# RWKV scan: one product of constants, 384 columns at full height, at each step of the chain

## The chip, the cores and the metric

The kernel runs as one program on one core of a Trainium2 chip. The metric is the device time of one execution in microseconds (us). Three runs of the kernel before took 2750.27, 2752.72 and 2759.83 us; the median is 2752.72. All data are 32-bit floats.

The engines: TensorE (PE) multiplies matrices and writes into PSUM, which has 8 banks of 512 columns on 128 partitions. VectorE (DVE) and ScalarE (ACT) work element by element, GpSimd (POOL) and SyncE (SP) issue transfers here. TensorE's matmuls need a load of weights first (PEld in the profile). A product of 32-bit operands appears as two MATMUL records.

## The reference

The model has two hybrid blocks, then a block with an RWKV mixer and one with latent attention. The change lies in the scan of the RWKV mixer: 512 tokens (256 of context, then 256 of input), 16 heads of 64, two directions. What it computes, cut to the core:

```python
def wkv_scan(r, logw, k, v, a, b, s0):
    tm = lambda t: jnp.moveaxis(t.astype(jnp.float32), 2, 0)

    def step(s, inp):
        r_t, lw_t, k_t, v_t, a_t, b_t = inp
        sa = jnp.einsum('dbhij,dbhj->dbhi', s, a_t)
        s = s * jnp.exp(lw_t)[..., None, :] + sa[..., None] * b_t[..., None, :] + v_t[..., None] * k_t[..., None, :]
        return s, jnp.einsum('dbhij,dbhj->dbhi', s, r_t)

    s_fin, y = lax.scan(step, s0, (tm(r), tm(logw), tm(k), tm(v), tm(a), tm(b)))
    return jnp.moveaxis(y, 0, 2), s_fin
```

## The kernel before

`stage_rwkv_scan` works through 8 rounds of 128 channels (n = 0 to 7), each with two heads (e) and two directions (d). The 512 tokens are cut into NCK = 16 chunks of LCH = 32. For each round, products of small tiles turn every chunk into a matrix GR that carries a state over the chunk; then a chain of steps c = 0 to 16 runs the state through the chunks in order.

The order of all work is a list, `scan_order`, which every engine walks in the same order and picks its own part from. For round i it has two parts. In the first, the solving of round i (`atok`, `akv`, `pq`, `gr`) is mixed with the gram products of round i + 1 and the reading out of round i - 1. In the second, the chain of round i is mixed with the triangular inverse of round i + 1 on VectorE (`inv`, 31 pieces, from 0.3 of the chain on) and with the preparation of round i + 2: two pairs of LoRA products (`lora`, L1553), sums, a small transpose and a spread for the norm of kk (`kk`, L1538, L1696, L1544) and two scans on VectorE. Rounds 0 to 5 have a later round i + 2 to prepare, rounds 6 and 7 have none, and round 7 has no inverse either.

A step c of the chain on TensorE: it waits for `u_done`, the scaling of step c - 1; `carried` (L1641) adds GR times the scaled state U to the bank c % 2 and raises `state_up`; `inner` (L1634) opens the other bank, (c + 1) % 2, with the part of the next chunk that needs no state; `read_state` (L1649) and `read_inner` (L1658) write the outputs of the chunk into banks 2 and 3. VectorE meanwhile waits for `state_up`, multiplies columns 0 to 127 of the bank by the decay (`rw_u`, L1965) and raises `u_done`. All these products use quarters of the array: 64 rows by 64 columns of weights, with 64 or 32 columns streamed, four to a group. The state's banks are k.psum[0] and k.psum[1]; the chain uses 128 of their 512 columns, and nobody reads the others while the chain runs.

`k.con` holds constants in SBUF: the identity in columns 0 to 127 (`ident`), all ones in the next 128, and a block matrix of ones in the next.

Of the kernel before, what the change touches and what calls it, by code (L numbers as in the profile page):

```python
# [20 lines left out]
P = 128  # L21
# [105 lines left out]
def const(k, name):  # L127
    return k.con[:, CON[name]:CON[name] + P]
# [1225 lines left out]
def stage_rwkv_scan(nc, k, a, lora, kept, o):  # L1354
# [14 lines left out]
    with ExitStack() as ctx:  # L1369
# [56 lines left out]
        ident, headones = const(k, "ident"), const(k, "headones")  # L1426
# [18 lines left out]
        def rows64(i):  # L1445
            return slice(64 * i, 64 * i + 64)
# [73 lines left out]
        def _(pe):  # L1520
# [108 lines left out]
            def inner(n, c):  # L1629

                h, c2 = c % 2, c // 2
                for d in range(2):
                    for e in range(2):
                        mm = pe.matmul(k.psum[h][rows64(e), 64 * d:64 * d + 64], BG[n % 2][d][rows64(h), c2, e, 0:64],  # L1634
                                       PQ[d][rows64(h), c2, e, 64:128], start=(d == 0), stop=(c == 0), skip_group_check=True)
                return mm

            def carried(n, c):
                for d in range(2):
                    for e in range(2):  # L1640
                        mm = pe.matmul(k.psum[c % 2][rows64(e), 64 * d:64 * d + 64], GR[d][rows64(e), c, 0:64],  # L1641
                                       U[rows64(e), c % 2, d, :], start=False, stop=True, skip_group_check=True)
                return mm

            def read_state(n, c):
                for d in range(2):
                    at = 256 * d + 32 * (c // 2)
                    for e in range(2):
                        mm = pe.matmul(k.psum[2 + c % 2][rows64(e), at:at + 32], U[rows64(e), c % 2, d, :],  # L1649
                                       GR[d][rows64(e), c, 64:96], start=(d == 0), stop=False, skip_group_check=True)  # L1650
                return mm

            def read_inner(n, c):
                h, c2 = c % 2, c // 2
                for d in range(2):
                    at = 256 * d + 32 * c2
                    for e in range(2):
                        mm = pe.matmul(k.psum[2 + h][rows64(e), at:at + 32], PQ[d][rows64(h), c2, e, 64:128],  # L1658
                                       BG[n % 2][d][rows64(h), c2, e, 64:96], start=(c == 0 and d == 0), stop=True,
                                       skip_group_check=True)  # L1660
                return mm

            def chain(n, c):
                if c == 0:
                    pe.wait_ge(gr_down, 8 * (n + 1))
                    if n:
                        pe.wait_ge(u_done, (NCK - 1) * n)
                        pe.wait_ge(ysum_done, n)
                        pe.wait_ge(step_up, (NCK + 1) * n)
                    inner(n, 0).then_inc(state_up, 1)  # L1670
                    inner(n, 1).then_inc(step_up, 1)
                    return
                pe.wait_ge(step_up, (NCK + 1) * n + c)
                if c < NCK:
                    pe.wait_ge(u_done, (NCK - 1) * n + c)
                    if c < NCK - 1:
                        carried(n, c).then_inc(state_up, 1)
                    if c + 1 < NCK - 1:
                        inner(n, c + 1)
                    read_state(n, c)  # L1680
                read_inner(n, c - 1).then_inc(step_up, 1)
# [7 lines left out]
            for item in items:  # L1689
# [33 lines left out]
                elif kind == "pq":  # L1723
                    solved(n, *item[2:])
                elif kind == "gr":
                    steps_made(n, *item[2:])
                elif kind == "chain":
                    chain(n, item[2])
                elif kind == "bonus" and item[2] == 0:
                    bonus_sums(n)  # L1730
                elif kind == "read" and item[2] == 1:
                    pe.wait_ge(ysum_done, n + 1)
                    pe.matmul(take(*item), cen, ysb, start=True, stop=True).then_inc(yc_up, 1)
                    free(ysq_done, n + 1, *item)
                elif kind == "read" and item[2] == 2:
                    pe.wait_ge(ysq_done, n + 1)
                    out = take(*item)
                    for q in range(4):
                        mm = pe.matmul(out[:, 2 * q:2 * q + 2], ysq[:, q * P:(q + 1) * P], half2[:, 0:2], start=True,
                                       stop=True)  # L1740
                    mm.then_inc(var_up, 1)
                    free(var_down, n + 1, *item)
                elif kind == "read" and item[2] == 3:
                    pe.wait_ge(yr_done, n + 1)
                    out = take(*item)
                    pe.transpose(out[0:8, 0:P], rst, ident).then_inc(yt_up, 1)
                    free(yt_down, n + 1, *item)
                elif kind == "read" and item[2] == 4:
                    pe.wait_ge(yt_down, n + 1)
                    spread(take(*item), rstT).then_inc(yb_up, 1)  # L1750
                    free(o_done, n + 1, *item)
# [825 lines left out]
```

## Time and profile before

| | us |
|---|---|
| median of three runs | 2752.72 |
| lowest, highest | 2750.27, 2759.83 |
| the profiled execution | 2753.79 |
| its span, first to last instruction | 2752.1 |
| TensorE busy with matmuls | 2289.5 (83%) |
| TensorE busy with weight loads | 1798.2 (65%) |
| VectorE busy | 983.9 (36%) |
| ScalarE busy | 523.1 (19%) |

Durations of single pieces come from the profiled execution, so sums are made against its 2753.79 us. Its mean granted TensorE clock is 0.848 of full speed. The scan takes the stretch from about 1700 to 2375 us. In the profile, "matmuls cover" means that at least one matmul was under way; several on different quarters of the array can overlap. Line numbers L... are those of kernel.py as below. "64\*64" ahead of a shape says how many rows and columns of the array a matmul used.

### The profile page before, as it was taken

Reading aid. Unit: us, or ns where it says so; the run is one execution under the profiler, and the core shown is the slowest. Engines: PE = TensorE matmul, PEld = TensorE weight load, DVE = VectorE, ACT = ScalarE, POOL = GpSimd, SP = SyncE. Lnnn points to the kernel's source line nnn. Section 1 sums busy time; section 2 is a strip of 40 time slices with the busy share of each in tenths; the row PEclk is TensorE's granted clock in tenths of the full one; section 3 lists DMA queues with packets and bytes.
Section 4 is the critical chain, followed back from the end, with each engine's and each line's share of the span. In section 5 each row is a group of like instructions: output and inputs, shape, how many; then the busy total and the mean of one; then the engine's idle time right before and its main releaser. Section 6 shows DMA issues by size and latency. Waiting matters only on the chain. (4 is left out here: it accounts for less than half of the span.)

```text
span 2752.1 us, 43845 instructions
## 1 busy us (share of the span) xinstructions
PE 2289.5 (83%) x18934; PEld 1798.2 (65%) x18934; DVE 983.9 (36%) x2209; ACT 523.1 (19%) x944; POOL 57.5 (2%) x84
## 2 busy tenths in 40 slices
PE   1999955798999876999579973988889889779797
PEld 1888854687888765888534432777777778536445
DVE  3224345402440562773341005335443343110243
ACT  1011122401000102000100013344433442000142
POOL 0000010000000300000000000000000000000000
PEclk9999977998999988999889985666756666689889
DMA  7455411325874311874212211111111110312100
GB/s 290 178 227 228 168 50 27 66 100 204 319 270 153 122 46 61 319 306 184 96 51 97 77 52 41 35 42 33 24 40 33 43 25 10 123 65 92 42 20 16
DMA packets 101929, 301.25 MB, mean 109 GB/s; under 512 B 71272, under 2 KB 79720, under 8 KB 83568
## 3 DMA queue, kind: packets, MB, share of 16 engines
q1 hardware_dynamic: 93808, 223.01, 24.0%
q0 software_dynamic: 7936, 75.50, 7.1%
q8 instruction: 149, 2.44, 0.4%
q14 instruction: 36, 0.29, 0.0%
HBM read 284.78 MB, written 13.71 MB: 108 GB/s over the span
## 5 line engine op out<-in xcount | busy, mean ns | idle before, releaser
L263 PE MATMUL bank<-h,ring 128*128 128x256 f32 x2944 | 646.5, 383 | 22.8 <-DVEq L967 15.3
L263 PEld LDWEIGHTS bank<-h,ring 128*128 128x128 f32 x2944 | 566.2, 192 | 104.0 <-DVEq L967 16.1
L263 PE MATMUL bank<-mixed,ring 128*128 128x512 f32 x384 | 165.0, 592 | 1.3 <-DVE mixed L1249 1.3
L877 PE MATMUL bank<-ffn_hidden,ring 128*128 128x256 f32 x704 | 152.4, 379 | 3.3 <-PEq L903 3.3
L877 PEld LDWEIGHTS bank<-ffn_hidden,ring 128*128 128x128 f32 x704 | 133.6, 190 | 22.2 <-issue 4.1
L263 PEld LDWEIGHTS bank<-mixed,ring 128*128 128x128 f32 x384 | 72.9, 190 | 93.5 <-issue 91.4
L156 DVE CUSTOM_DVE_ANT_0 next_w<-next_w,next_vec,par 128x1024 f32<-128x1024 f32 x96 | 120.3, 1281 | 11.3 <-DMA next_w<-in_mod_stream 11.3
L1658 PE MATMUL bank<-ring 64*64 64x32 f32 x1024 | 110.3, 289 | 0.6
L1634 PE MATMUL bank<-ring 64*64 64x64 f32 x960 | 99.3, 300 | 8.3 <-ACT rw_gr L1856 8.3
L1649 PE MATMUL bank<-rw_gr,rw_u 64*64 64x32 f32 x960 | 98.4, 283 | 0.5
L1658 PEld LDWEIGHTS bank<-ring 64*64 64x64 f32 x1024 | 93.3, 208 | 1.7 <-PE bank L1658 1.7
L1641 PE MATMUL bank<-rw_u,rw_gr 64*64 64x64 f32 x896 | 75.1, 315 | 22.5 <-DVE rw_u L1965 18.2
L889 DVE SCALAR_TENSOR_TENSOR x<-bank,mod,x 128x256 f32<-128x256 f32 x24 | 10.0, 477 | 231.6 <-PE bank L877 231.6
L1597 PE MATMUL bank<-ring 32*32 32x128 f32 x1024 | 89.0, 341 | 4.0 <-DMA ring<-rw_mt_kept 2.2
L1965 DVE TENSOR_TENSOR rw_u<-bank,rw_lam 128x128 f32<-128x128 f32 x120 | 34.8, 290 | 153.8 <-PE bank L1641 95.6
L1641 PEld LDWEIGHTS bank<-rw_u,rw_gr 64*64 64x64 f32 x896 | 55.4, 205 | 52.4 <-issue 28.7
L1597 PEld LDWEIGHTS bank<-ring 32*32 32x32 f32 x1024 | 74.2, 137 | 20.8 <-issue 14.4
L1634 PEld LDWEIGHTS bank<-ring 64*64 64x64 f32 x960 | 79.3, 195 | 9.7 <-ACT rw_gr L1856 9.3
L1649 PEld LDWEIGHTS bank<-rw_gr,rw_u 64*64 64x64 f32 x960 | 83.2, 206 | 1.5 <-PE bank L1658 1.5
L877 PE MATMUL bank<-y,ring 128*128 128x256 f32 x384 | 83.1, 379 | 0.8 <-PEq L679 0.8
L401 DVE COPY y<-bank 128x512 f32<-128x512 f32 x20 | 13.8, 692 | 186.1 <-PE bank L263 186.1
L877 PEld LDWEIGHTS bank<-y,ring 128*128 128x128 f32 x384 | 72.9, 190 | 10.9 <-issue 1.1
(362 smaller groups left out, 3353.9 us busy)
## 6 DMA issues: line engine op xcount, KB each, us to landing
ring<-in_stream SPq DMA_DIRECT2D x89, 2048.0 KB, 8.1
next_w<-in_mod_stream POOLq DMA_DIRECT2D x24, 2048.0 KB, 10.3
ctx<-in_mod_rest POOLq DMA_DIRECT2D x16, 1024.0 KB, 7.5
rwkv_projections<-proj_out POOLq DMA_DIRECT2D x8, 1024.0 KB, 6.7
rw_rkvg<-rwkv_projections SPq DMA_DIRECT2D x8, 1024.0 KB, 4.8
y<-bias_table SPq DMA_DIRECT2D x48, 128.0 KB, 4.8
rw_at<-rw_at_kept SPq DMA_DIRECT2D x16, 256.0 KB, 4.2
rw_at_kept<-ring SPq DMA_DIRECT2D x32, 64.0 KB, 1.9
```

What stands on the lines that cost most here:

```text
L156: return nc.vector.tensor_tensor_reduce(products, w, vec, 1.0, bias, ALU.mult, ALU.add, out)
L263: mm = pe.matmul(out, ring_tile(k, n, kt, i * P), rhs[kt], start=start and kt == kts[0], stop=stop and kt == kts[-1])
L401: nc.vector.tensor_copy(dst, k.psum[2 * (j % 2)].rearrange("p (i t) -> p i t", i=2)).then_inc(stored_dve, 1)
L877: mm = pe.matmul(k.psum[grp * 4 + i][:, 0:T], ring_tile(k, n, kt, i * P), rhs[part * KT + kt], start=(part == 0 and kt == 0), stop=(part = ...
L889: nc.vector.scalar_tensor_tensor(k.x[:, m, :], k.psum[m][:, 0:T], gain[:, m:m + 1], k.x[:, m, :], ALU.mult, ALU.add)
L1597: pe.matmul(out[brows(h), j * P:(j + 1) * P], BG[n % 2][d][brows(h), c2, e, 96:128], AV[brows(h), c2, e, :], start=True, stop=True)
L1634: mm = pe.matmul(k.psum[h][rows64(e), 64 * d:64 * d + 64], BG[n % 2][d][rows64(h), c2, e, 0:64], PQ[d][rows64(h), c2, e, 64:128], start=(d ...
L1641: mm = pe.matmul(k.psum[c % 2][rows64(e), 64 * d:64 * d + 64], GR[d][rows64(e), c, 0:64], U[rows64(e), c % 2, d, :], start=False, stop=Tru ...
L1649: mm = pe.matmul(k.psum[2 + c % 2][rows64(e), at:at + 32], U[rows64(e), c % 2, d, :], GR[d][rows64(e), c, 64:96], start=(d == 0), stop=Fal ...
L1658: mm = pe.matmul(k.psum[2 + h][rows64(e), at:at + 32], PQ[d][rows64(h), c2, e, 64:128], BG[n % 2][d][rows64(h), c2, e, 64:96], start=(c == ...
L1965: v.tensor_tensor(U[:, (c + 1) % 2, :, :], k.psum[c % 2][:, 0:P].rearrange("p (d v) -> p d v", d=2), lam[:, n % 2, :, c + 1:c + 2].to_broa ...
```

## The change

One line in `chain`: after `carried` of step c, and before `inner` of step c + 1, TensorE gets a product of the identity with 384 columns of the constants. It uses all 128 rows and columns of the array and writes columns 128 to 511 of the bank (c + 1) % 2, which nobody reads. It stands under the condition of `inner`, so in steps 1 to 13 of each round.

```diff
                     if c < NCK - 1:
                         carried(n, c).then_inc(state_up, 1)
                     if c + 1 < NCK - 1:
+                        pe.matmul(k.psum[(c + 1) % 2][:, P:512], ident, k.con[:, 0:384], start=True, stop=True)
                         inner(n, c + 1)
                     read_state(n, c)
                 read_inner(n, c - 1).then_inc(step_up, 1)
```

The order of TensorE's instructions at the start of a round's chain (L1641 `carried`, L1634 `inner`, L1649 `read_state`, L1658 `read_inner`, L1538 the sums of squares, L1553 a LoRA pair), before:

```order
458 L1538 MATMUL bank<-rw_half,rw_sq 128x2 x4
459 L1641 MATMUL bank<-rw_u,rw_gr 64x64 x4
460 L1634 MATMUL bank<-ring 64x64 x4
461 L1649 MATMUL bank<-rw_gr,rw_u 64x32 x4
462 L1658 MATMUL bank<-ring 64x32 x4
463 L1641 MATMUL bank<-rw_u,rw_gr 64x64 x4
464 L1634 MATMUL bank<-ring 64x64 x4
465 L1649 MATMUL bank<-rw_gr,rw_u 64x32 x4
466 L1658 MATMUL bank<-ring 64x32 x4
467 L1553 MATMUL bank<-lora,rw_w 128x512 x2
```

The same place with the change, where L1679 is the new product:

```order
458 L1538 MATMUL bank<-rw_half,rw_sq 128x2 x4
459 L1641 MATMUL bank<-rw_u,rw_gr 64x64 x4
460 L1679 MATMUL bank<-con 128x384
461 L1634 MATMUL bank<-ring 64x64 x4
462 L1649 MATMUL bank<-rw_gr,rw_u 64x32 x4
463 L1658 MATMUL bank<-ring 64x32 x4
464 L1641 MATMUL bank<-rw_u,rw_gr 64x64 x4
465 L1679 MATMUL bank<-con 128x384
466 L1634 MATMUL bank<-ring 64x64 x4
467 L1649 MATMUL bank<-rw_gr,rw_u 64x32 x4
468 L1658 MATMUL bank<-ring 64x32 x4
469 L1553 MATMUL bank<-lora,rw_w 128x512 x2
```

Nothing else moved: each step has its one product behind the state's four, and the other engines' orders are the same.

## Rows read from the trace of the kernel before

**Rows 1.** The page: TensorE's granted clock in tenths, 40 slices of the span.

```profile
PEclk9999977998999988999889985666756666689889
```

**Rows 2.** Stretches: from:to, length, busy time per engine (instructions), PEclk, DMA share, GB/s.

```profile
1758.00:2372.00 614.00, 544.97 (x10468) 470.20 (x10467) 256.42 (x754) 216.69 (x392) 0.00 (x0) 0.66 0.14 28
```

**Rows 3.** Line L1965, steps 1 to 14 of rounds 4, 2, 6 and 7.

```profile
L1965 DVE TENSOR_TENSOR rw_u<-bank,rw_lam x14: 266/292/293, 2101.8 to 2136.0; 128x128 f32<-128x128 f32 x14
...
L1965 DVE TENSOR_TENSOR rw_u<-bank,rw_lam x14: 266/292/292, 1933.5 to 1961.8; 128x128 f32<-128x128 f32 x14
...
L1965 DVE TENSOR_TENSOR rw_u<-bank,rw_lam x14: 291/292/293, 2274.6 to 2300.0; 128x128 f32<-128x128 f32 x14
...
L1965 DVE TENSOR_TENSOR rw_u<-bank,rw_lam x14: 291/292/292, 2344.8 to 2369.2; 128x128 f32<-128x128 f32 x14
```

**Rows 4.** In order of time, TensorE, round 4: start, length, instruction, count.

```profile
2099.95 1.17 PE L1538 MATMUL bank<-rw_half,rw_sq 128*128 128x2 f32 x8 [0.41 <-ACT rw_sq L1785]
2101.05 0.58 PE L1641 MATMUL bank<-rw_u,rw_gr 64*64 64x64 f32 x5
...
2103.04 0.37 PE L1641 MATMUL bank<-rw_u,rw_gr 64*64 64x64 f32 x2
...
2104.89 2.08 PE L1553 MATMUL bank<-lora,rw_w 64*128 64x512 f32 x4
2106.89 0.58 PE L1641 MATMUL bank<-rw_u,rw_gr 64*64 64x64 f32 x5
```

**Rows 5.** In order of time, round 7, steps 1 and 2.

```profile
2344.30 0.35 PE L1641 MATMUL bank<-rw_u,rw_gr 64*64 64x64 f32 x5 [0.45 <-DVE rw_u L1965]
...
2344.78 0.29 DVE L1965 TENSOR_TENSOR rw_u<-bank,rw_lam 128x128 f32<-128x128 f32 x1 [0.63 <-PE bank L1641]
...
2345.46 0.27 PE L1641 MATMUL bank<-rw_u,rw_gr 64*64 64x64 f32 x2
```

**Rows 6.** In order of time, VectorE, round 4, scalings of steps 8 to 14.

```profile
2119.66 0.29 DVE L1965 TENSOR_TENSOR rw_u<-bank,rw_lam 128x128 f32<-128x128 f32 x1
...
2124.72 0.29 DVE L1965 TENSOR_TENSOR rw_u<-bank,rw_lam 128x128 f32<-128x128 f32 x1
...
2126.82 0.29 DVE L1965 TENSOR_TENSOR rw_u<-bank,rw_lam 128x128 f32<-128x128 f32 x1
...
2130.07 0.29 DVE L1965 TENSOR_TENSOR rw_u<-bank,rw_lam 128x128 f32<-128x128 f32 x1
...
2134.68 0.29 DVE L1965 TENSOR_TENSOR rw_u<-bank,rw_lam 128x128 f32<-128x128 f32 x1
...
2136.02 0.29 DVE L1965 TENSOR_TENSOR rw_u<-bank,rw_lam 128x128 f32<-128x128 f32 x1
```

**Rows 7.** Stretches of rounds 2, 4, 7 and of 2155 us.

```profile
1940.00:1950.00 10.00, 9.33 (x214) 7.77 (x211) 6.72 (x27) 3.44 (x6) 0.00 (x0) 0.98 0.01 4
2101.00:2136.00 35.00, 31.81 (x455) 27.01 (x455) 18.66 (x66) 6.16 (x9) 0.00 (x0) 0.50 0.01 1
...
2155.00:2160.00 5.00, 5.00 (x126) 4.38 (x120) 1.78 (x3) 4.25 (x8) 0.00 (x0) 0.96 0.01 3
2344.00:2346.00 2.00, 1.63 (x54) 1.55 (x55) 0.49 (x3) 0.00 (x0) 0.00 (x0) 1.00 0.00 0
2350.00:2365.00 15.00, 14.48 (x246) 13.40 (x244) 2.04 (x7) 0.00 (x0) 0.00 (x0) 0.50 0.01 2
```

**Rows 8.** In order of time, TensorE, round 2, the LoRA pairs.

```profile
1936.62 2.08 PE L1553 MATMUL bank<-lora,rw_w 64*128 64x512 f32 x4
...
1943.01 0.27 PE L1641 MATMUL bank<-rw_u,rw_gr 64*64 64x64 f32 x2
...
1944.06 1.13 PE L1553 MATMUL bank<-lora,rw_w 64*128 64x512 f32 x4
1945.12 0.38 PE L1641 MATMUL bank<-rw_u,rw_gr 64*64 64x64 f32 x5
```

**Rows 9.** In order of time, TensorE, behind round 4's chain.

```profile
2144.86 0.39 PE L1566 MATMUL bank<-rw_xa,ring 64*64 64x64 f32 x4 [4.54 <-DVE rw_xa L1900]
...
2152.77 1.91 PE L1733 MATMUL bank<-rw_ysb,rw_cen 128*128 128x512 f32 x2
```

## The prediction

> **What bounds the kernel now.** I number the scan's eight rounds 0 to 7 and the steps of a round's chain c = 0 to 16. I began with the page: in its row of the granted clock, slices 25 to 35 of 40 are the one long stretch at 5 to 7 tenths [rows 1], and that is the scan. The table of stretches says how much: between 1758 and 2372 us, matmuls cover 545 of 614 us and the mean clock is 0.66 [rows 2]. The clock has two levels, 1.2 and 2.4 GHz, which the rows show as 0.50 and 1.00, so a mean of 0.66 is a third of the time high.
>
> Next the chain of one round, on VectorE, whose scaling (L1965) closes each step. Round 4 needs 34.2 us from step 1 to step 14, round 2 only 28.3, rounds 6 and 7 25.4 and 24.4 [rows 3]. The steps themselves come from the order of time on TensorE: at the low clock a plain step takes 2103.04 - 2101.05 = 1.99 us [rows 4], at the high clock 2345.46 - 2344.30 = 1.16 us [rows 5]. In both the engine hardly waits; the one wait for a scaling in these rows is 0.45 us in front of step 1 of round 7 [rows 5]. So in steps 1 to 8 TensorE sets the pace. From step 9 on, in rounds 0 to 5, it does not: VectorE works through the triangular inverse between the scalings, and 2.10, 3.25, 4.61 (for two) and 1.34 us pass between them, with no idle time of VectorE in front of them [rows 6]. There an extra product lies beside VectorE's work as far as TensorE's step stays shorter.
>
> When does the clock change? In round 7 it is high at first (1.00 in 2344 to 2346) and then 0.50, with matmuls in 14.5 of 15 us [rows 7]. The only wide products in the chains are the LoRA pairs (L1553, two in each of rounds 0 to 5): behind the one at 1936.62 the clock was 0.98 from 1940 to 1950, which makes round 2's short chain; behind the one at 2104.89 it did not rise, since 2101 to 2136 has a mean of 0.50 [rows 4, 7, 8]. It is 0.96 in 2155 to 2160, behind a product of 512 columns at full height that ran from 2152.77 to 2154.68 [rows 7, 9]. So small tiles alone did not bring it up; what stood before a rise was work over all rows of the array.
>
> The Trainium skill ("TensorE: Matmul & The Clock Gate", What's actually happening) says that the default is throttled and activity releases it. If busy time were what counts, rows 7 would show the high level; the trace disagrees, 0.50 with matmuls in 97% of the time, so what kind of matmul runs matters. By the page's rule read as it stands, the clock would follow any product put in; that is the third rival.
>
> **The change part by part.** One product per step 1 to 13, 13 x 8 = 104 in all, between the state's product (L1641) and the next step's inner products (L1634). It waits for nothing new and frees nothing; no DMA, no work of another engine. What queues behind it on TensorE: inner(c+1), the two reads, then the state's product of step c+1. The scaling of step c has its semaphore before it, so the product delays the scaling of step c+1, not of c.
>
> Price of one at each clock. The nearest row is the LoRA pair: two products of 512 columns, 64 rows each, side by side, thus a full-height one of 512. At the low clock the step that holds it takes 2106.89 - 2103.04 = 3.85 us, 1.86 more than the plain one [rows 4]; 384 columns are 0.75 of that, 1.40 us. At the high clock 1945.12 - 1943.01 = 2.11, 0.95 more [rows 5, 8]; times 0.75 is 0.71 us. Lower bound: no cost, where VectorE is late. Upper bound: the lone 512-column product, 1.91 us, and 0.2 for a weight load that isn't hidden, times 0.75 = 1.6 low, some 0.9 high [rows 9]. I take 1.40 and 0.71, since the pair stands in this very place of the chain. A plain step becomes 3.39 us low and 1.87 high. Note: high with the product is hardly shorter than low without it (1.99). The most that the change can win is therefore small.
>
> The skill's page "TensorEngine Tiling (Array Packing)" (Key Properties) adds that changing the tiling mode drains TensorE. The LoRA pair changes mode as well, so that its 1.86 us already hold it; if the full array cost one more drain each way, the upper bound would apply, some 20 us more in all.
>
> What the clock does. In rounds 0 to 5 it falls about step 0 (behind eight tiny products, L1538, in front of step 1 [rows 4]), before the first new product runs. Then the product is 1.40 us in a step of 3.39, less than the LoRA pair's 1.86 in 3.85 at 2104.89, which brought nothing: I expect no rise in steps 1 and 2. The first LoRA pair with new products on both sides is more full-height work than the pair at 1936.62, behind which it rose; so there I expect the rise. It then holds: the product is 0.71 us in a high step of 1.87. Between the scalings of steps 10 and 11 VectorE's 3.25 us leave TensorE idle for 1.4 us, and the clock may fall again, in about half the rounds. Rounds 6 and 7 arrive high and should stay.
>
> Sum for round 4, steps 1 to 14 (scaling to scaling): 3.39 low; 5.25 with the pair (3.85 + 1.40); 2.6 for the rise within the step; 1.87 twice; 2.82 (1.87 + 0.95); 1.87; 4.03 for the step with the spread L1544 (5.06 low [rows 6], less 0.83 for the plain step's gain, less 0.91 for the spread's, taken like the pair's 1.86 - 0.95, plus 0.71); 2.10, 3.25, 4.61 covered; 2.6 for the last, half high at 1.87, half low at 3.39. Together 36.3 against 34.2: +2.1. Rounds 0, 1, 3, 5 alike, so 5 x 2.1 = 10.5. Round 2 loses its luck: 36.3 - 28.3 = +8.0. Rounds 6 and 7: 13 x 1.87 = 24.3, against 25.4 and 24.4: -1. Sum +18.
>
> Some chain will not behave: a step of 3.39 us with its product repeats almost unchanged, so a round that misses the rise stays low. All low, it is ten steps of 3.39, two of 5.25 with pairs and one of 6.46 with the spread, 50.9 us: 16.7 more than before, 14.6 more than forecast. I count one such round in eight: +15. Behind the chain nothing is won: TensorE waits 4.54 us for VectorE there and is low again [rows 9].
>
> Forecast: 2753.8 + 18 + 15 = 2787 for the profiled execution. It took 2753.8 (span 2752.1 and 1.7 around it), 1.1 above the median of 2752.7; against that, 2786.
>
> **Rivals.**
> Low throughout: the products are never enough, pair or not. For it: the pair at 2104.89 brought nothing. Cost: rounds 0, 1, 3, 4, 5 each +16.7, round 2 50.9 - 28.3 = +22.6, rounds 6 and 7 13 x 3.39 = 44.1, +18.7 and +19.7; together +144: 2898. Against: the rise at 1940 came with less.
> Hidden: the clock as before and the products in TensorE's waits. Against: at the low clock the engine waits under 0.2 us a step (0.52 of 15 us over seven steps and a half [rows 7]), and 104 x 1.40 = 146 us don't go into that. A middle case stands here too: what the products cost is given back by the clock. Either ends within 8 us of before, 2745 to 2761.
> High throughout, and faster: the first product in step 1 already lifts or holds the clock in every round. Rounds 0 to 5 then take six plain ones of 1.87, two of 2.82, 4.03, and 9.96 for the covered ones, 30.9 with the last at 1.87 among the six: 5 x -3.3, round 2 +2.6, rounds 6 and 7 -1: -15, and with a product a tenth cheaper in some 80 steps another -5: 2734 to 2739. What decides it is step 1, whether the product's share at the low clock is enough. Against: it is under the LoRA pair's at 2104.89. The rule of the Trainium skill's page on TensorE's clock, named above, would come out at this same time.
>
> **How the numbers follow.** Partly high as forecast, from +8 to +80 according to how many rounds stay low (none to four of eight, and a product at its upper bound): 0.58. Low throughout or nearly: 0.10. Hidden or balanced: 0.15. High throughout: 0.17. A change of over 0.3% (8 us) is what this measurement can tell. So faster 0.17, same 0.15, slower 0.68. The range: 2738 takes in most of the high case, 2850 four or more rounds low; the likeliest case's own range is 2761 to 2833.
>
> **What would show it.** L1679 with 104 products, two records each; steps of 3.4 us with clock 0.50 and of 1.9 us with 1.00; in rounds 0 to 5 the change from the one to the other behind the first L1553; steps 9 to 13 unchanged; rounds 6 and 7 at 1.00. It is wrong if steps 1 and 2 already run in 1.9 us (then faster), if the pairs lift nothing, or if a high step takes over 2.1 us (the product dearer than 0.9).

## The result: 5% slower, and the profile after

The changed kernel takes 2888.31 us (median of four runs, 2881.24 to 2915.25) against 2754.94 for the one before (four runs, 2750.27 to 2759.83): a ratio of 1.0502, 95% interval 1.0429 to 1.0575. I had forecast 2786, range 2738 to 2850. The direction was right; the size is four times the forecast, and above the range. The profiled execution took 2894.58 (span 2892.9), 140.8 more than that of before.

The page shows the product as one group of 208 records, two for each of the 104, with no idle time in front of it. What answers to [rows 1] is the granted clock, which is at 5 to 8 tenths in slices 23 to 35.

```profile
PE 2444.7 (85%) x19142; PEld 1845.1 (64%) x19142; DVE 983.8 (34%) x2209; ACT 522.3 (18%) x944; POOL 57.3 (2%) x84
...
PEclk9999977999999978998899756675666866599889
...
L1679 PE MATMUL bank<-con 128*128 128x384 f32 x208 | 152.5, 831 | 0.0
...
L1634 PEld LDWEIGHTS bank<-ring 64*64 64x64 f32 x960 | 50.6, 185 | 107.7 <-issue 98.4
```

The last line is new: the weight loads of the inner products (L1634) now stand behind 98.4 us of idle time put down to "issue"; before, the whole group had 9.7 us in front of it, nearly all for ScalarE. This idle time isn't itself the price: E1 below has 0.6 us of it and still pays 0.73 us a step, and E9 has 89.3 us of it (in front of the loads of L1641) with a cheaper product.

The table of stretches for the scan (answering to [rows 2]) has it growing from 614 to 754 us, at a mean clock of 0.67, nearly what it was. That mean hides the change: it is now high in other places.

```profile
1758.00:2512.00 754.00, 697.26 (x10799) 513.07 (x10794) 256.54 (x754) 219.26 (x397) 0.00 (x0) 0.67 0.12 25
```

The scalings, now L1966, steps 1 to 14: round 2, round 4, round 6, round 7. They answer to [rows 3].

```profile
L1966 DVE TENSOR_TENSOR rw_u<-bank,rw_lam x14: 251/292/293, 1965.4 to 2020.0; 128x128 f32<-128x128 f32 x14
...
L1966 DVE TENSOR_TENSOR rw_u<-bank,rw_lam x14: 290/292/293, 2182.4 to 2226.7; 128x128 f32<-128x128 f32 x14
L1966 DVE TENSOR_TENSOR rw_u<-bank,rw_lam x14: 290/292/293, 2370.4 to 2418.6; 128x128 f32<-128x128 f32 x14
L1966 DVE TENSOR_TENSOR rw_u<-bank,rw_lam x14: 291/292/293, 2463.0 to 2511.5; 128x128 f32<-128x128 f32 x14
```

Round 2 went from 28.3 to 54.6 us, round 4 from 34.2 to 44.3, rounds 6 and 7 from 25.4 and 24.4 to 48.2 and 48.5. With step 0 to step 1 counted as well (from the scaling of step 0 to that of step 14), all rounds are:

```
us, scaling 0 to scaling 14       round 0     1     2     3     4     5     6     7    sum
before                            35.69 36.08 31.57 36.73 36.47 36.78 26.37 25.30  265.0
after                             56.95 40.80 56.39 57.45 47.83 40.84 49.09 49.38  398.7
```

That is +133.7. The stretches between the rounds add 2.9 (349.7 against 346.9), the first scaling comes 5.7 later, and 1.5 is won behind the last. So the change is in the chains, as forecast, and nearly nowhere else.

The clock in four stretches: round 7 from step 1 on; round 2, all its steps; round 1 behind its first LoRA pair.

```profile
2463.00:2511.00 48.00, 47.12 (x440) 30.13 (x442) 3.79 (x13) 0.00 (x0) 0.00 (x0) 0.50 0.00 1
...
1964.00:2020.00 56.00, 55.36 (x484) 34.88 (x485) 18.73 (x66) 6.16 (x9) 0.00 (x0) 0.51 0.01 1
...
1885.00:1905.00 20.00, 18.48 (x277) 12.00 (x277) 12.25 (x45) 3.43 (x5) 0.00 (x0) 1.00 0.01 2
```

Behind the first LoRA pair the clock rose in rounds 1, 4 and 5 and did not in 0, 2 and 3. Rounds 6 and 7 arrived high (step 1 takes 0.92 us in both) and fell in step 2. The order of time on TensorE, round 7 at the low clock, then round 4 at the high one:

```profile
2476.90 0.69 PE L1641 MATMUL bank<-rw_u,rw_gr 64*64 64x64 f32 x8
2477.52 1.65 PE L1679 MATMUL bank<-con 128*128 128x384 f32 x2
2479.10 0.40 PEld L1634 LDWEIGHTS bank<-ring 64*64 64x64 f32 x6 [1.08 <-issue]
...
2480.66 0.69 PE L1641 MATMUL bank<-rw_u,rw_gr 64*64 64x64 f32 x8
...
2196.60 0.45 PE L1641 MATMUL bank<-rw_u,rw_gr 64*64 64x64 f32 x8
2196.98 0.91 PE L1679 MATMUL bank<-con 128*128 128x384 f32 x2
...
2198.78 0.45 PE L1641 MATMUL bank<-rw_u,rw_gr 64*64 64x64 f32 x8
```

A step is 3.76 us low and 2.18 high. Against 1.98 and 1.16 of before the product costs 1.78 and 1.02; the forecast had 1.40 and 0.71. The same place in the kernel before shows what may lie behind a part of it:

```profile
2352.75 0.32 PE L1641 MATMUL bank<-rw_u,rw_gr 64*64 64x64 f32 x2
2352.78 0.31 PE L1634 MATMUL bank<-ring 64*64 64x64 f32 x1
```

There L1641 and L1634 run in turns. Now the product stands between the two: L1641 finishes by itself, and the first weight load of L1634 comes only at the product's end. In the rows of round 7 a low step of 3.76 us falls into 0.62 from the start of L1641 to that of the product, 1.58 from there to L1634, and 1.56 to the next L1641. So the product holds TensorE for 1.58 us, and the rest of the step takes 2.18 in place of 1.98.

### The profile page after: what moved, and what is told of

Read it like the earlier page. It is cut to its first block and busy times, and to the rows that moved or that the text cites. A ratio compares the mean times of both kernels' runs of the same rounds, so it can differ in the third digit from the quotient of the medians.

```text
span 2892.9 us, 44261 instructions
## 1 busy us (share of the span) xinstructions
PE 2444.7 (85%) x19142; PEld 1845.1 (64%) x19142; DVE 983.8 (34%) x2209; ACT 522.3 (18%) x944; POOL 57.3 (2%) x84
## 5 line engine op out<-in xcount | busy, mean ns | idle before, releaser
L1679 PE MATMUL bank<-con 128*128 128x384 f32 x208 | 152.5, 831 | 0.0
L1966 DVE TENSOR_TENSOR rw_u<-bank,rw_lam 128x128 f32<-128x128 f32 x120 | 34.8, 290 | 279.8 <-PE bank L1641 224.3
L1634 PEld LDWEIGHTS bank<-ring 64*64 64x64 f32 x960 | 50.6, 185 | 107.7 <-issue 98.4
L1658 PE MATMUL bank<-ring 64*64 64x32 f32 x1024 | 104.3, 279 | 0.6
L1649 PE MATMUL bank<-rw_gr,rw_u 64*64 64x32 f32 x960 | 94.4, 275 | 0.5
L1658 PEld LDWEIGHTS bank<-ring 64*64 64x64 f32 x1024 | 87.6, 197 | 1.7 <-PE bank L1658 1.7
L1649 PEld LDWEIGHTS bank<-rw_gr,rw_u 64*64 64x64 f32 x960 | 79.7, 196 | 1.5 <-PE bank L1658 1.5
L1599 PE MATMUL bank<-ring,con 32*32 32x64 f32 x1024 | 79.2, 275 | 0.0
L1641 PE MATMUL bank<-rw_u,rw_gr 64*64 64x64 f32 x896 | 70.8, 301 | 9.7 <-DVE rw_u L1966 4.5
L2066 PE MATMUL bank<-mla_h,ring 128*128 128x256 f32 (+1 forms) x240 | 67.3, 444 | 12.5 <-PEq L190 12.5
```

What stands on the lines that cost most here:

```text
L1599: mm = pe.matmul(out[krows(h), j * P + 64:(j + 1) * P], ident[krows(h), krows(h)], AV[krows(h), c2, e, 0:64], start=True, stop=True)
L1679: pe.matmul(k.psum[(c + 1) % 2][:, P:512], ident, k.con[:, 0:384], start=True, stop=True)
L1966: v.tensor_tensor(U[:, (c + 1) % 2, :, :], k.psum[c % 2][:, 0:P].rearrange("p (d v) -> p d v", d=2), lam[:, n % 2, :, c + 1:c + 2].to_broa ...
L2066: mm = pe.matmul(out, ring_tile(k, n, kt, i * P), rhs[kt], start=(kt == 0), stop=(kt == KT - 1))
```

## The experiments

Two questions were open: why the product is dearer than the forecast (a price of changing from 64x64 tiles to the full array and back, or the place), and why the clock did not rise, and fell in rounds 6 and 7. All times are medians (of two runs in E1 to E3, E5, E6, E8 and E9, of five in E4, four in E7, six in E10 and E11); each ratio is against the kernel before on the same chip, with its 95% interval. As the clock is not the same in every round, I read prices from single steps and behaviour from the rounds. "Low" and "high" are clock 0.50 and 1.00.

**E1, 8 columns in place of 384.** In the change's place:

```diff
+ pe.matmul(k.psum[(c + 1) % 2][:, P:P + 8], ident, k.con[:, 0:8], start=True, stop=True)
```

> The product as in the change, full height, but 8 columns instead of 384. Theory A (fixed price: at the low clock 1.78 us a product against 1.28 of streaming, so some 0.50 us go for the change of the array's mode and a load of weights that nothing hides): low steps of 1.99 + 0.50 = 2.5 us, some 104 x 0.5 less what VectorE covers, about +40 us, 2790. Theory B (the price goes with the columns, full height streams slower than 2 passes of 384 at 1.2 GHz): 8 columns cost nothing, steps of 2.0, 2755.

2824.13, ratio 1.0272 (1.0227 to 1.0317). The order of time in round 7, low:

```profile
2426.49 0.59 PE L1679 MATMUL bank<-con 128*128 128x8 f32 x2
...
2426.60 0.29 DVE L1966 TENSOR_TENSOR rw_u<-bank,rw_lam 128x128 f32<-128x128 f32 x1 [2.40 <-PE bank L1641]
...
2429.19 0.59 PE L1679 MATMUL bank<-con 128*128 128x8 f32 x2
```

A low step is 2.71 us: 0.73 for a product that streams next to nothing. So there is a fixed price in this place. From 8 to 384 columns a step grows by 1.05 us (2.71 to 3.76), just as the product's own row does (0.59 to 1.65), so the rest is the same at any width. The rows split the 0.73 us: 0.52 from the product's start to L1634, and 0.20 more in the rest of the step, as with 384 columns. The expectation, 0.50 us a product and 2790 us, was too low. The product doesn't bring the clock up either: every round is low from its third step on, as all but round 2 were before (35.6 and 35.8 us in rounds 6 and 7, 42.0 to 43.8 in the others, sum 330.0).

**E2 and E3, the same columns as 64x64 tiles.** In a step, between its wait for the reads of the step before (`step_up`) and that for the scaling (`u_done`); E3 has both calls, E2 one:

```diff
+ def fill(b, at, cols):
+     for e in range(2):
+         pe.matmul(k.psum[b][rows64(e), at:at + cols], ident[rows64(e), rows64(e)],
+                   k.con[rows64(e), 0:cols], start=False, stop=True, skip_group_check=True)
...
+ if 2 <= c < NCK - 1:
+     fill(c % 2, P, 384)
+     fill(c % 2, P, 384)
```

> In place of the full-height product, two products on quarters of the array that together cover all rows, 64 rows x 64 columns of weights, 384 columns streamed, side by side; no change of mode. They stand in steps 2 to 14 before the state's product. Theory A: 1.28 us and hardly more, low steps of 3.3 to 3.4, high ones of 1.85 to 1.9. Theory B: 1.78, steps of 3.76 and 2.18 again. On the clock: if the share of work over all rows in a step decides, the cheaper product has the larger share (1.28 of 3.35 against 1.28 of 3.76), and more rounds rise behind the LoRA pairs than the three of six that did. Time about 2790 to 2840 with A, 2885 with B.

> The two quarter products twice in each of steps 2 to 14. If the share of work over all rows decides on the clock: 2.56 of a low step of 4.6 us; the clock rises in every round within two or three steps, rounds 6 and 7 stay high, and steps 3 to 8 take some 2.5 us. Time near 2800, although twice as much was added. If the clock doesn't answer to these products: every step low, 4.6 us, some 2990.

E2: 2814.45, ratio 1.0237 (1.0196 to 1.0278). A low step is 3.27 (price 1.29), a high one 1.83 (0.66). E3: 2805.49, ratio 1.0204 (1.0158 to 1.0251): with twice the work no slower, though the 9 us between the two medians are within the noise. In E2 all of rounds 0 to 5 rose (0, 2, 4 and 5 behind the first LoRA pair, 1 and 3 behind the second), and rounds 6 and 7 ran low. One stretch of E2's round 7, one of E3's round 7:

```profile
2395.00:2430.00 35.00, 34.27 (x385) 23.96 (x384) 3.15 (x11) 0.00 (x0) 0.00 (x0) 0.50 0.01 1
```

```profile
2394.00:2419.00 25.00, 24.34 (x421) 15.93 (x415) 2.92 (x10) 0.00 (x0) 0.00 (x0) 1.00 0.01 2
```

TensorE is covered by matmuls to 98% and 97% in these two, and one is at the low level, the other at the high. In E3 every round rose by step 3. The busy share does not tell the levels apart. What differs between E2 and E3 is the wide work, by which I mean long products over all rows: once in a step it left rounds 6 and 7 low, twice it lifted them. Such work can be done in 64x64 tiles, so the full-height form isn't needed for it.

**E4, no product in the chain, one in each wait of step 0.** The waits of step 0 that concern other things are moved ahead of that for the masked Gram blocks (`gr_down`):

```diff
+ fill(3, 0, 384)
  pe.wait_ge(gr_down, 8 * (n + 1))
  inner(n, 0).then_inc(state_up, 1)
  inner(n, 1).then_inc(step_up, 1)
+ fill(3, 0, 192)
```

> No product in the steps at all; two pairs of quarter products per round in TensorE's waits around step 0: 384 columns while it waits for the last copy before the chain, 192 columns while it waits for the first scaling. Theory C (the clock falls because of the waits around step 0, and a chain of high steps of 1.16 us then holds itself): rounds 6 and 7 high throughout, 16 us instead of 25.4 and 24.4; rounds 0 to 5 high for some of steps 1 to 8, up to 6 us less each: 2710 to 2740. Theory D (the chain's small tiles can't hold the high clock, whatever stands before them): it falls in step 2 or 3 as before, 2750 to 2757.

2714.59, ratio 0.9863 (0.983 to 0.9896): 1.4% faster than the kernel before. Its profiled execution took 2749.2, the others 2707 to 2721, so its trace serves for single steps and rounds only. The products in round 4, in order of time; before, TensorE waited 0.98 us for ScalarE in front of this round's first L1634 and 0.41 us in front of L1538:

```profile
2113.66 0.86 PE L1665 MATMUL bank<-con 64*64 64x384 f32 x4
...
2115.00 0.53 PE L1665 MATMUL bank<-con 64*64 64x192 f32 x4
```

Rounds 2 and 4 took 26.9 us (high to step 8), round 6 21.5 and round 7 16.3; rounds 0, 1, 3 and 5, with 35.5 to 36.5, were within 1.3 us of before. So a round whose beginning is bridged can keep the high clock throughout, in round 7 with matmuls in 15.0 of 16 us and no wide work in any step.

```profile
2351.00:2367.00 16.00, 15.01 (x436) 13.53 (x435) 3.85 (x14) 0.00 (x0) 0.00 (x0) 1.00 0.01 3
```

**E5, E4 and the change's product together.** The edit is E4's with the change's line.

> The change's full-height products in steps 1 to 13, and the two pairs of quarter products in the waits around step 0. Theory E (in a low step of 3.76 us the product is too small a share to lift the clock, in a high one of 2.18 us it is enough to hold it, so a round keeps the clock it starts with): rounds 6 and 7 now high from start to end, 0.9 + 13 x 2.18 = 29.3 us each instead of 49.1 and 49.4; rounds 0 to 5 high from step 1 where they start high (about half of them, some 36 us). Time some 60 us less than the change: 2810 to 2840. Theory F (the full-height product itself brings the clock down, whatever the start): rounds 6 and 7 low again behind step 1, 49 us, 2880.

2789.67, ratio 1.0154 (1.0093 to 1.0215). Round 7's scalings and clock:

```profile
L1973 DVE TENSOR_TENSOR rw_u<-bank,rw_lam x14: 290/292/292, 2391.4 to 2419.7; 128x128 f32<-128x128 f32 x14
```

```profile
2391.00:2420.00 29.00, 28.13 (x466) 18.68 (x466) 4.08 (x14) 0.00 (x0) 0.00 (x0) 1.00 0.01 2
```

Rounds 6 and 7 are 29.2 us in place of 49.1 and 49.4, at the high clock to the end, with the very product that ran at the low clock in the changed kernel. Rounds 0 to 5 are 40.6, 34.8, 36.3, 34.8, 36.4 and 57.8: the first five were high in step 1 and stayed so at least to step 9, the last was low from its first step to its end. So with this product in it a chain can stay at either clock. In rounds 6 and 7 what stands before it decided which; to be high in step 1 isn't enough, since both were so in the changed kernel too. The time came out below the 2810 to 2840 of Theory E, as five of rounds 0 to 5 were high and not about half.

**E6, the change's line twice.**

> The change's product twice in each of steps 1 to 13. The second needs no new mode and no new weights: at the low clock + 1.28 us to the first's 1.78, steps of 5.04. If the share of full-height work in a step decides on the clock: 2.56 of 5.04 us is more than what failed (1.28 of 3.76, and 1.28 of 3.27 with quarters, rounds 6 and 7) and less than what rose (2.56 of 4.55, quarters twice). If it rises, steps of 2.8 us, rounds 6 and 7 about 38 us each, time near 2850, less than with half the work; if not, every step low at 5.04, rounds 6 and 7 66 us each, some 3040.

2835.23, ratio 1.032 (1.0279 to 1.0361): 53 us less than with the line once. A low step is 5.04 and a high one 2.82, so the second product adds 1.28 us low and 0.64 high, less than the first with 1.78 and 1.02. Every round was high by step 4 (rounds 6 and 7 39.0 and 37.6 us, sum 345.6).

```profile
2416.00:2450.00 34.00, 33.20 (x438) 21.29 (x434) 3.52 (x13) 0.00 (x0) 0.00 (x0) 1.00 0.01 1
```

**E7, E4 and one more product before step 1.** In `key_values`, before its waits, for the last of them:

```diff
+ if (d, e) == (1, 0):
+     if n:
+         pe.wait_ge(step_up, (NCK + 1) * n)
+     fill(0, P, 384)
```

> As e4_bridge (products only in the waits around step 0), and one more pair of quarter products, 384 columns, in TensorE's wait of 0.84 us before the key-value products of the second direction, where the clock fell in rounds 1, 3 and 5 of e4_bridge's profile and made their chains start low. Theory C: with that wait bridged all eight chains start high; rounds 0 to 5 take about 27 us to step 14 as rounds 2 and 4 did (26.9), 16.3 in round 7. Time 2680 to 2705, 10 to 30 below e4_bridge. Rival: the fall there has another cause than the wait (eight products of 8 rows stand there too), then as e4_bridge, 2715.

2712.54, ratio 0.9859 (0.9811 to 0.9906), no better than E4. Rounds 1 and 2 began high and lost it at step 3, round 3 at step 2, and round 4 began low (sum 239.9); round 1 as a whole:

```profile
1837.00:1869.00 32.00, 28.82 (x428) 24.12 (x426) 17.83 (x64) 5.84 (x8) 0.00 (x0) 0.53 0.01 2
```

The expectation failed: a high start isn't enough in rounds 0 to 5. What is missing there stays open. It can't be wide work alone: rounds 2 and 4 of E4 have the same steps and held the clock to step 8, and round 7 held it through all its steps (16.3 us) without any.

**E8, half the height.** 64 rows by 128 columns of weights, in the change's place:

```diff
+ r = (c + 1) % 2
+ pe.matmul(k.psum[r][:, P:512], ident[rows64(r), :], k.con[rows64(r), 0:384], start=True, stop=True)
```

> In the change's place, one product of 64 rows (those of the inner products behind it) and 128 columns of weights, 384 columns streamed. It changes the array's mode, but leaves the other rows free. If the change of mode costs the 0.50 us beyond streaming: low steps of 3.76 again. If it is the full height (nothing can be loaded or streamed beside it): below 3.4, since the other rows' work lies beside it. The clock: half the rows, a smaller share, so low throughout also behind the LoRA pairs; some 2860 to 2890.

2934.78, ratio 1.0682 (1.064 to 1.0725), above the 2860 to 2890 expected. A low step is 3.75 us, the same as with the full height, and the clock is low in all eight rounds, behind both LoRA pairs too (sum 440.7).

```profile
2511.45 1.64 PE L1680 MATMUL bank<-con 64*128 64x384 f32 x2
...
2515.19 1.64 PE L1680 MATMUL bank<-con 64*128 64x384 f32 x2
```

So the product costs the same at half the height, and the clock seems to depend on it: at equal time and columns, with half the rows, the three rises of the changed kernel are gone. As one and the same kernel rises in some rounds and not in others, one profile of each shows this less firmly than the price.

**E9, the full product at the LoRA pair's place.** The step's beginning, before the wait for the scaling:

```diff
+ if 2 <= c < NCK - 1:
+     pe.matmul(k.psum[c % 2][:, P:512], ident, k.con[:, 0:384], start=False, stop=True,
+               skip_group_check=True)
```

> The change's full-height product of 384 columns in another place: in steps 2 to 14, before the wait for the step before, where the LoRA pair stands and TensorE starts afresh anyway. Theory G (its 0.50 us beyond streaming belong to the place: between the state's and the inner products it breaks two groups that ran side by side, and here there is nothing to break): the pair's price, 0.75 x 1.87 = 1.40 us low and 0.71 high, steps of 3.4 and 1.87 as predicted, chains of 36 to 38 us where the clock rises behind the first pair, 49 us less where it fails; time 2780 to 2840. Theory H (any change of the array's mode costs 0.50 us): 3.76 and 2.18 again, 2885. The clock: rounds 6 and 7 fall in step 2 as with the change.

2824.38, ratio 1.0252 (1.0205 to 1.0298). The order of time in round 6, low, and two scalings of round 7, high:

```profile
2342.03 1.65 PE L1674 MATMUL bank<-con 128*128 128x384 f32 x2
2343.61 0.37 PE L1641 MATMUL bank<-rw_u,rw_gr 64*64 64x64 f32 x2
2343.64 0.37 PE L1634 MATMUL bank<-ring 64*64 64x64 f32 x1
...
2421.34 0.29 DVE L1968 TENSOR_TENSOR rw_u<-bank,rw_lam 128x128 f32<-128x128 f32 x1 [1.60 <-PE bank L1641]
...
2423.23 0.29 DVE L1968 TENSOR_TENSOR rw_u<-bank,rw_lam 128x128 f32<-128x128 f32 x1 [1.60 <-PE bank L1641]
```

L1641 and L1634 run in turns again. A low step is 3.42 and a high one 1.89: 1.44 and 0.73, where the forecast had 1.40 and 0.71. So the place accounts for what the forecast lacked. The rows show how. The product holds TensorE for 1.58 us here too (2342.03 to 2343.61), just as in the change; at the high clock it is 0.84 us in both. What differs is the rest of the step: 1.85 us here, 2.18 in the change, 1.98 before. Here it is shorter than before, because the product runs where L1641's first weight load used to wait about 0.2 us for the end of L1658; in the change it is longer, because L1641 and L1634 no longer overlap. The clock rose in all of rounds 0 to 5 (rounds 0, 2, 4 behind the first pair, 1, 3, 5 behind the second) and stayed high in round 7, against the expectation that both last rounds would fall; round 6 was low (45.7 us). The chains sum to 313.2, +48 against before. Between the rounds there are 364.5 us, 17.6 more than before, and 17 of these lie in three of the seven stretches: 53.5, 57.0 and 56.9 us at a mean clock of 0.74, 0.69 and 0.69, where before had 50.4, 49.9 and 49.8 at 0.77. So the clock varies outside the chains too.

**E10 and E11, E7 with small products to hold the clock.** In rounds 0 to 5, behind the wait for the scaling, 128 columns in steps 1 to 8 (E10) or 384 in steps 1 and 2 (E11):

```diff
+ if n < KT - 2 and c < 9:      # E10
+     fill(c % 2, P, 128)
+ if n < KT - 2 and c < 3:      # E11
+     fill(c % 2, P, 384)
```

> As e7_bridge_two, and in steps 1 to 8 of rounds 0 to 5 a pair of quarter products of 128 columns (0.43 us low, 0.21 high) after the wait for the step before. If more work over all rows holds the high clock where rounds 1, 2 and 3 of e7_bridge_two lost it in step 3: steps of 1.4 us, chains of 28 to 30 us in at least four of rounds 0 to 5 instead of 34 to 37; time 2685 to 2705. If not: 8 x 0.43 = 3.4 us more in each of the six rounds, 2725 to 2735.

> As e7_bridge_two, and in steps 1 and 2 of rounds 0 to 5 a pair of quarter products of 384 columns (1.28 us low, 0.65 high). If the clock is lost there only at the start of the chain: 1.3 us more in a round that starts high, and it stays high to step 9: chains of 28 us, time 2685 to 2705. If it is lost anyway: 2 x 1.28 us more in those rounds, 2720 to 2730.

E10: 2703.78, ratio 0.9818 (0.9791 to 0.9845). E11: 2700.81, ratio 0.9803 (0.9777 to 0.9829). The two don't differ clearly from each other, and E10's interval overlaps that of E7; in the traces the chains sum to 218.9 and 219.2 us against E7's 239.9. E11's scan, and its round 1:

```profile
1759.00:2320.00 561.00, 500.15 (x10596) 420.57 (x10597) 256.32 (x754) 218.05 (x393) 0.00 (x0) 0.77 0.15 31
...
1849.00:1865.00 16.00, 14.22 (x316) 11.19 (x313) 8.72 (x35) 5.98 (x8) 0.00 (x0) 0.99 0.02 4
```

Rounds 1 to 5 take 28.2 to 28.5 us (before 31.6 to 36.8), rounds 6 and 7 21.7 and 16.3; round 0 stayed low (39.5). The sum is 219.2 against 265.0.

## Why the prediction was wrong

**What held.** The scan is bound by TensorE at one of two clocks; the cost is in the chains (133.7 of 140.8 us); one product a step, 104 in two records each, that nothing waits for by name; VectorE's stretches cover it in steps 9 to 13 where the clock is high (round 5 of after: 2.11, 3.25, 2.61, 1.99); a high share of busy time alone doesn't lift the clock, and more wide work in a step does (E2, E3).

**The sum taken apart.** The forecast's +33 was for the steps 1 to 14, which went from 248.7 us to 383.1 over the eight rounds (the sums above less the distances from scaling 0 to 1): +134.4. With the forecast's prices but the clock as it came (rounds 0, 2, 3 low at 50.9 each, rounds 6 and 7 low at 44.1, rounds 1, 4, 5 with the rise at 36.3) they would sum to 349.8, +101. So of the 140.8 us the forecast had 33; 68 more are the clock, 33 more the price (8 of them in round 4, of which about 5 are its clock, which fell again at step 9: rounds 1 and 5 took 39.1 us, round 4 44.3), and 6 lie outside these steps. The next two points are the 68 and the 33.

**The step that failed first: "What the clock does".** I wrote that there, behind the first LoRA pair, "I expect the rise", and that rounds 6 and 7 "arrive high and should stay". Three of six rounds missed the rise, and both last ones fell in their second step. The allowance of one low round in eight should have been five. The reasoning behind it was a comparison at a 3.39 us step, and the real step is 3.76: the same wide work in a longer step. That the price works through the clock as well is my reading of it, not shown by a run that changes the step's length alone. E9, whose low step is 3.42, fits: all six rounds rose, and round 7 stayed high. But three of them rose behind the second pair only, and round 6 was low, so even then "should stay" was too sure. E5 shows the other half: in rounds 6 and 7 the same product at the same price runs high to the end once the waits of step 0 are filled. What I had not seen is that with a product this size the chain can stay at either clock for all its steps; I had priced one low round, not both outcomes for each of the eight.

**The term mis-sized: "Price of one at each clock".** I took the pair's price times 0.75 "since the pair stands in this very place of the chain". It doesn't: the pair stands ahead of the wait for the scaling, where the engine starts afresh anyway, and the change stands between L1641 and L1634, which otherwise run in turns. E9 (1.44 and 0.73 at the pair's place) against the change (1.78 and 1.02) puts 0.34 and 0.29 us on the place. At the low clock 0.20 of the 0.34 is the rest of the step that grew in the change, and 0.13 the wait that the product fills in E9. In these two traces the place is worth 85 of the 133.7 us in the chains, through price and clock together, since E9's +48 is what is left at the other place; in the medians of the whole time it is 64 us. The upper bound of 1.6 and 0.9 came from a product that stands alone [rows 9]. It matches the 1.58 for which the product holds TensorE, and lacked the longer rest of the step. The text said what would be wrong if "a high step takes over 2.1 us"; it takes 2.18.

The page "TensorEngine Tiling (Array Packing)" of the Trainium skill (Key Properties) says that changing the tiling mode drains TensorE. The forecast cited it and reasoned that the pair's price "already hold it". The trace is compatible with the rule: the full-array product holds TensorE for 1.58 us in the change and in E9 alike, 0.30 more than the 1.28 that a second one adds in E6, and the 64x64 tiles of E2 hold it for 1.33. But no run separates a change of mode from the other things that are new with this product. E8 pays the same as the full height, and its weights are 128 columns wide as well; quarter tiles between L1641 and L1634, or a change of mode with narrow weights, were not tried. So what the 0.30 us are stays open, and the forecast's reason held as far as it went: the pair's price did hold them. What it lacked was the neighbours.

**The rivals.** "Low throughout" named 2898 and 1.40 a product; the time came within 10 us of it, but by another way: five rounds low, at a dearer product. I gave it 0.10, which was too little: round 7 of before, which fell from high to low by itself [rows 7], spoke for it. "High throughout" and "Hidden" are excluded for this edit, yet E11 shows what the first was after: 53 us less than before (2700.81 against 2753.73), with products in the waits and in tiles of the mode that runs there. How the clock comes to miss in one round and not in another (rounds 1 and 2 of the changed kernel start alike, 1.75, then 3.68 and 3.71 us, 5.63) stays open. Their first pairs and the second scaling behind each:

```profile
1879.76 2.08 PE L1553 MATMUL bank<-lora,rw_w 64*128 64x512 f32 x4
...
1884.99 0.29 DVE L1966 TENSOR_TENSOR rw_u<-bank,rw_lam 128x128 f32<-128x128 f32 x1 [2.19 <-PE bank L1641]
...
1972.00 2.08 PE L1553 MATMUL bank<-lora,rw_w 64*128 64x512 f32 x4
...
1978.51 0.29 DVE L1966 TENSOR_TENSOR rw_u<-bank,rw_lam 128x128 f32<-128x128 f32 x1 [3.47 <-PE bank L1641]
```

The waits for L1641 in front of them are 2.19 and 3.47 us: round 1 is at the high clock there, round 2 is not.

## What to carry to other kernels

Take the price of an added instruction from a row in the same position relative to its neighbours and waits: one that separates two groups that ran in turns cost 0.3 us more here than the same one ahead of a wait. Then split the step into the time for which the new instruction holds the engine and the rest; here the first was the same at both places, and the rest was not. Work added to lift a clock belongs into the engine's waits ahead of the stretch (here in the tile mode that runs there); in E4, E5 and E11 it cost less than it gave, and it decided the clock of rounds 6 and 7. Where a stretch can run at either of two clocks, count its rounds by how they start, and price both outcomes with a chance for each instead of allowing for one mishap.

## What the runs showed of the hardware that was not expected

- More work can take less time: the change's line twice took 2835 us, once 2888. Quarter tiles twice (2805) were no slower than once (2814).
- A full-array product of 8 columns between groups of 64x64 tiles costs 0.73 us at the low clock.
- The same chain with the same product ran 13 steps at 2.18 us (E5, rounds 6 and 7) or 12 at 3.76 (the changed kernel, the same rounds), with no difference but in what stands ahead of it.
- At 97% to 98% of time covered by matmuls the clock was low in some stretches (E2) and high in others (E3); in the kernel with half the rows no round rose (E8).
- A chain of small tiles alone held the high clock through all its steps (round 7 of E4, E7 and E11: 16.3 us, clock 1.00), where before the change it fell in its third step.
- A product of 64x128 weights at 384 columns takes as long as one of 128x128: 1.64 and 1.65 us.
- Wherever the full-array product stands, it holds TensorE for 1.58 us low and 0.84 high (the change, E9).
